# A chunked delta-rule block: the 16x16 diagonal blocks in one strided transfer each way, and their inversion placed ahead of other VectorE work

## The reference

```
l_mat = where(strict, (kbeta @ k.T) * decay, 0)
a_mat = eye(CHUNK) + l_mat
sol   = triangular_solve(a_mat, [v * beta, kbeta * exp(gcum)], lower, unit_diagonal)
v_new = u - w @ state
o     = q_dec @ state + qk @ v_new
state = state * g_last + k_dec.T @ v_new
```

```
o_a = rms_norm(o_a) * silu(z);   mix = concat(o_a, o_b) @ w_out
x   = x + rms_norm(mix);         h = rms_norm(x)
```

## Time and profile before

| | us |
|---|---|
| median of 3 runs | 1429.09 (1427.49 to 1430.75) |
| the profiled execution | 1428.89 |
| its span | 1427.1 |
| of it `mix`, about | 278 to 680 |
| PE busy over the span | 1287.3 (90%) |
| DVE busy | 709.1 (50%) |
| ACT busy | 398.0 (28%) |
| POOL busy | 150.8 (11%) |

### The profile page before, as it was taken

One profiled execution on the slowest core, in us unless ns is written; L12 is line 12 of the kernel. 1 busy time (PEld: TensorE's weight loads), 2 busy tenths in 40 slices (PEclk: granted clock), 3 DMA queues, 4 the chain that ended last, 5 costly groups with the idle time before them and its releaser, 6 DMA issues.

```text
span 1427.1 us, 17527 instructions
## 1 busy us (share of the span) xinstructions
PE 1287.3 (90%) x6360; PEld 1088.5 (76%) x6360; DVE 709.1 (50%) x1075; ACT 398.0 (28%) x744; POOL 150.8 (11%) x184
## 2 busy tenths in 40 slices
PE   5899999647588988878899999999999999999995
PEld 4788888537577878776688888888888888888884
DVE  5232444324756655652653544536362635445358
ACT  5121222235334434422442122122212121221312
POOL 1121000021222123211300000000000000000005
PEclk9999999867699999999899999999999999999998
DMA  7220322272113223112311101011111101010123
GB/s 237 99 100 38 105 74 76 67 266 70 64 38 100 85 97 98 40 47 94 103 60 58 59 29 59 33 56 58 59 42 46 59 29 59 29 59 29 42 91 133
DMA packets 80650, 106.65 MB, mean 75 GB/s; under 512 B 17727, under 2 KB 62559, under 8 KB 80607
## 3 DMA queue, kind: packets, MB, share of 16 engines
q1 hardware_dynamic: 80607, 106.09, 22.4%
HBM read 82.97 MB, written 23.10 MB: 74 GB/s over the span
## 4 chain that ended last, share of the span: by engine, by line
PE 49%; POOL 1%; DVE 1%; issue 1%; ACT 0%; POOLq 0%
PE f_ps_up L2074 11%; PE f_ps_up L2075 11%; PE f_ps_up L2076 11%; PE sums L2092 5%; PE sums L2093 5%; PE sums L2094 5%; POOL stage L1801 1%; POOL f_conv L1801 0%; DVE split L1999 0%; POOL f_stat L2058 0%; DVE f_w_lo L1940 0%; ACT f_w_hi L1872 0%; POOLq L1708 0%; DVE f_conv L2012 0%; DVE h_t L1992 0%
## 5 line engine op out<-in xcount | busy, mean ns | idle before, releaser
L2074 PE MATMUL f_ps_up<-split,f_w_hi 128*128 128x512 f32 x704 | 275.7, 392 | 2.8 <-DVE split L1999 2.8
L2075 PE MATMUL f_ps_up<-split,f_w_hi 128*128 128x512 f32 x704 | 275.3, 391 | 0.0
L2076 PE MATMUL f_ps_up<-split,f_w_lo 128*128 128x512 f32 x704 | 275.1, 391 | 0.0
L1945 DVE SCALAR_TENSOR_TENSOR f_conv<-f_ps_up,f_taps,f_conv 128x1023 f32<-128x1023 f32 x88 | 112.8, 1281 | 275.2 <-ACT f_conv L1876 269.7
L2074 PEld LDWEIGHTS f_ps_up<-split,f_w_hi 128*128 128x128 f32 x704 | 132.9, 189 | 31.4 <-DVE split L1999 2.0
L2076 PEld LDWEIGHTS f_ps_up<-split,f_w_lo 128*128 128x128 f32 x704 | 133.0, 189 | 27.7
L2075 PEld LDWEIGHTS f_ps_up<-split,f_w_hi 128*128 128x128 f32 x704 | 133.0, 189 | 27.5
L1876 ACT ACTIVATE f_conv<-f_ps_up,f_taps 128x1024 f32<-128x1024 f32 x44 | 53.1, 1208 | 326.1 <-PE f_ps_up L2076 326.1
L1957 DVE TENSOR_TENSOR h_t<-sums,h_t 128x512 f32<-128x512 f32 x176 | 116.2, 685 | 37.3 <-PE sums L2094 37.2
L2092 PE MATMUL sums<-f_w_hi,f_y_hi 128*128 128x512 f32 x320 | 124.5, 389 | 0.0
L2093 PE MATMUL sums<-f_w_lo,f_y_hi 128*128 128x512 f32 x320 | 124.5, 389 | 0.0
(11 more groups left out here) (274 smaller groups left out, 2060.0 us busy)
## 6 DMA issues: line engine op xcount, KB each, us to landing
stage<-in_w_up SPq DMA_DIRECT2D x22, 1024.0 KB, 5.1
stage<-in_w_down SPq DMA_DIRECT2D x11, 1024.0 KB, 4.9
raw<-in_w_in SPq DMA_DIRECT2D x6, 1024.0 KB, 6.3
qkv<-xin SPq DMA_DIRECT2D x11, 512.0 KB, 3.2
rows<-row SPq DMA_DIRECT2D x8, 644.0 KB, 3.2
stage<-rows SPq DMA_DIRECT2D x8, 644.0 KB, 5.4
xin<-in_x SPq DMA_DIRECT2D x8, 512.0 KB, 4.8
raw<-in_w_in SPq DMA_DIRECT2D x8, 512.0 KB, 5.6
```

The costliest lines, as they stand in the source:

```text
L1945: op = dve.scalar_tensor_tensor(conv[:, q, k:S], ps_up[:, q % 2, 0:S - k], taps[:, bass.ds(ct + (FTAPS - 1 - k) * 2 * FT, 1)], conv[:, q, ...
L2074: pe.matmul(bank, hi, h_hi[:, k, cols], start=(k == 0), stop=False)
L2075: pe.matmul(bank, hi, h_lo[:, k, cols], start=False, stop=False)
L2076: op = pe.matmul(bank, lo, h_hi[:, k, cols], start=False, stop=(k == KD - 1))
```

## The change

1. `on_diagonal` now describes the diagonal blocks of all four heads in one access pattern. For this the scratch tensors are laid out by head (128x128 numbers of a head, then a gap of 128), so that whole tiles go in and out in pieces of 128 numbers (512 bytes) instead of 512 (2 KB). `load_blk` is one transfer instead of four, `store_xs` two instead of eight.
2. The one count for all of `store_xs` and the one for `load_inv` become two each: blocks may be stored after operation 16, turned blocks after 17; `a_off` waits for `inv` only, and the first `a_inv` for `inv_t`.
3. On VectorE `solve` stands right behind `a_add` of level 6, with `c_out` of the first half between its parts 1 and 2. `b_state` and `b_o`, `d_norm`, `a_qk`, `a_bv` and the second `c_max` come behind it. `d_lo` stands ahead of the first `c_max`. On ScalarE `d_hi` stands ahead of `a_turn` of level 5.
4. In `ffn`, the eight loads of the residual count on two semaphores (four each) instead of four (two each).

```diff
-        def on_diagonal(m, h):
-            pitch = BASE * H * P + BASE
-            return m[0:NB * pitch].rearrange("(b a) -> b a", a=pitch)[:, 0:BASE * H * P].rearrange(
-                "b (r h j) -> b r h j", h=H, j=P)[:, :, h, 0:BASE]
+        def on_diagonal(m):
+            return m[0:H * NB * (BASE * P + BASE)].rearrange("(g a) -> g a", a=BASE * P + BASE)[:, 0:BASE * P].rearrange(
+                "g (r j) -> g r j", j=P)[:, :, 0:BASE]
+        def whole(m):
+            return m.rearrange("(h a) -> h a", h=H)[:, 0:P * P].rearrange("h (p j) -> p h j", j=P)
...
             def load_blk(u):
-                ready((low_out, u, 16), (xs_out, u - 1, 128))
-                for h in range(H):
-                    sp.dma_start(blk[h * NB:(h + 1) * NB, 0:BASE * BASE].rearrange("p (r c) -> p r c", c=BASE),
-                                 on_diagonal(scratch["low"], h)).then_inc(blk_in.sem, 16)
+                ready((low_out, u, 16), (xs_out, u - 1, 16), (xs_t_out, u - 1, 16))
+                sp.dma_start(blocks_of(blk), on_diagonal(scratch["low"])).then_inc(blk_in.sem, 16)
             def store_xs(u):
-                ready((solved, u, SOLVE), (inv_in, u - 1, 32))
-                for m, blocks in ((scratch["inv"], blk), (scratch["inv_t"], products)):
-                    for h in range(H):
...
+                ready((solved, u, SOLVE - 1), (inv_in, u - 1, 16))
+                sp.dma_start(on_diagonal(scratch["inv"]), blocks_of(blk)).then_inc(xs_out.sem, 16)
+                ready((solved, u, SOLVE), (inv_t_in, u - 1, 16))
+                sp.dma_start(on_diagonal(scratch["inv_t"]), blocks_of(products)).then_inc(xs_t_out.sem, 16)
             def load_inv(u):
...
+                ready((xs_out, u, 16), (level, u - 1, L_INV[6]))
+                sp.dma_start(inv[:], whole(scratch["inv"])).then_inc(inv_in.sem, 16)
+                ready((xs_t_out, u, 16), (full["b0"], u - 1, 2))
+                sp.dma_start(inv_t[:], whole(scratch["inv_t"])).then_inc(inv_t_in.sem, 16)
...
                 if a:
+                    solve(t + 1, (0, 1))
+                    c_out(t + 1, 1 - par, 0)
+                    solve(t + 1, (2,))
+                if b:
+                    b_state(t, par)
+                    b_o(t)
                 if e:
                     d_norm(t - 2)
...
             def a_inv(t, n):
                 if n == FIRST:
+                    after(pe, inv_t_in, t)
...
-        s_xr = [sem(f"f_xr{n}") for n in range(T // 2)]
+        s_xr = [sem(f"f_xr{n}") for n in range(2)]
```

More of the change, by code:

```diff
@@ L667, in mix_block @@
         solved = tally("solved", SOLVE)
-        low_out, blk_in, xs_out, inv_in = tally("low_out", 16), tally("blk_in", 64), tally("xs_out", 128), tally("inv_in", 32)
+        low_out, blk_in = tally("low_out", 16), tally("blk_in", 16)
+        xs_out, xs_t_out, inv_in, inv_t_in = (tally(n, 16) for n in ("xs_out", "xs_t_out", "inv_in", "inv_t_in"))
         st_set, o1_set, o_set = tally("st_set"), tally("o1_set"), tally("o_set")
@@ L705, in corners @@
                 "p g (i j) -> p g i j", j=BASE)
-        def on_diagonal(m, h):
-            pitch = BASE * H * P + BASE
-            return m[0:NB * pitch].rearrange("(b a) -> b a", a=pitch)[:, 0:BASE * H * P].rearrange(
-                "b (r h j) -> b r h j", h=H, j=P)[:, :, h, 0:BASE]
-        scratch = {n: nc.dram_tensor(n + "_blocks", (P * (H * P + 1),), F32, kind="Internal").ap() for n in ("low", "inv", "inv_t")}
+        def on_diagonal(m):
[3 more added lines that the diff above has]
+            return m.rearrange("(h a) -> h a", h=H)[:, 0:P * P].rearrange("h (p j) -> p h j", j=P)
+        scratch = {n: nc.dram_tensor(n + "_blocks", (H * (P * P + P),), F32, kind="Internal").ap() for n in ("low", "inv", "inv_t")}
         w_rows = io["w_out"].rearrange("o (k p) n -> p (o k) n", p=P)
@@ L778, in store_x @@
                 sp.dma_start(res_flat[bass.ds(at, P * D)].rearrange("(p n) -> p n", p=P), x[:]).then_inc(x_out.sem, 16)
+            blocks_of = lambda m: m[:, 0:BASE * BASE].rearrange("g (r c) -> g r c", c=BASE)
             def store_low(u):
-                ready((low_set, u, 1), (blk_in, u - 1, 64))
-                sp.dma_start(tile_of(scratch["low"]), flat(low[:])).then_inc(low_out.sem, 16)
+                ready((low_set, u, 1), (blk_in, u - 1, 16))
+                sp.dma_start(whole(scratch["low"]), low[:]).then_inc(low_out.sem, 16)
@@ L797, in load_inv @@
+                ready((solved, u, SOLVE), (inv_t_in, u - 1, 16))
+                sp.dma_start(on_diagonal(scratch["inv_t"]), blocks_of(products)).then_inc(xs_t_out.sem, 16)
             def load_inv(u):
-                ready((xs_out, u, 128), (level, u - 1, L_INV[6]), (full["b0"], u - 1, 2))
-                sp.dma_start(flat(inv[:]), tile_of(scratch["inv"])).then_inc(inv_in.sem, 16)
-                sp.dma_start(flat(inv_t[:]), tile_of(scratch["inv_t"])).then_inc(inv_in.sem, 16)
+                ready((xs_out, u, 16), (level, u - 1, L_INV[6]))
@@ L821, in _ @@
             for m in (scratch["inv"], scratch["inv_t"]):
-                sp.dma_start(tile_of(m), flat(state[:])).then_inc(s_load, 16)
+                sp.dma_start(whole(m), state[:]).then_inc(s_load, 16)
             sp.wait_ge(s_load, LOADS)
@@ L1107, in step @@
                     a_dect(t + 1, 1 - par)
+                if d:
+                    d_hi(t - 1)
                 if b:
                     a_turn(t, 5)
-                if d:
-                    d_hi(t - 1)
                 if e:
@@ L1213, in solve @@
                     after(dve, blk_in, u)
-                    after(dve, xs_out, u - 1)
+                    after(dve, xs_t_out, u - 1)
                     then(dve.memset(blk[:].rearrange("p (r a) -> p r a", a=BASE + 1)[:, :, 0], 1.0), 1)
@@ L1386, in step @@
                     a_low(t + 1, 1 - par)
-                    c_max(t + 1, 0)
                 if d:
                     d_lo(t - 1)
+                if a:
+                    c_max(t + 1, 0)
                 if b:
@@ L1399, in step @@
                 if a:
-                    c_out(t + 1, 1 - par, 0)
                     a_qk(t + 1)
                     a_bv(t + 1, 1 - par)
[L1403 to L1407, removed]
                     c_max(t + 1, 1)
-                    solve(t + 1, (2,))
                 if b:
@@ L1797, in residual @@
             eng.wait_ge(s_norm, t + 1)
-            eng.wait_ge(s_xr[t // 2], 32)
+            eng.wait_ge(s_xr[t // 4], 64)
             if t >= T - 2:
@@ L1861, in _ @@
             for t in range(4, T):
[L1862 removed]
+                sp.dma_start(res_tile(t), io["res"][t]).then_inc(s_xr[t // 4], 16)
             for t in range(T):
```

6 lines of the change are left out of this document (2 added, 4 removed).

## The result

| | before | after |
|---|---|---|
| device time, median | 1429.09 us | 1413.55 us |
| range of five runs | 1427.49 to 1430.92 | 1408.22 to 1417.64 |
| profiled execution: its time; its span; mean granted clock | 1428.9; 1427.1; 0.951 | 1413.55; 1411.7; 0.954 |

The ratio is 0.9889, with an interval of 0.9859 to 0.9919. The change is faster by 15.5 us, where 30 were forecast. 1413.6 lies 8.6 us above the forecast's own range (1391 to 1405) and just above the wide one (1391 to 1413).

What follows compares the result with a forecast made beforehand. In `mix`, TensorE's waits were taken as the limit, worst for the inverse blocks. Steps -1 to 1 +0.3, 2 to 5 -18.1, 6 -3.9, 7 -8.7: -30.4 from 1428.9, so 1399 us; own range 1391 to 1405, wide 1391 to 1413.

Steps and rivals of the forecast that it cites:

- The wait for the inverse blocks: In steady steps of `mix`, TensorE's wait at `a_off` and the lowered clock behind it go: gain 4.3 us.
- Level 4: In steady steps, a new TensorE wait of 0.9 us ahead of `a_trinv`: loss 0.9.
- `d_lo`: TensorE's wait of 1.45 us for `d_lo` goes in steady steps, but L1515 comes only 1.0 earlier: gain 1.0.
- steps 6 and 7: Step 6 of `mix` was to shorten by 3.9 us, and step 7, without part a, by 8.7.
- The blocks in steps 2 to 5: VectorE waits only 0.1 to 0.2 us for the blocks at `solve`, upper bound 1.3; these steps gain 18.1 together.
- late blocks: Rival: `load_blk` with 512 pieces is slow, each microsecond past 2.2 to landing costing the step one: 1440 us, chance 0.04.
- The lowered clock: Rival: new TensorE waits of 0.9, 0.8 and 0.5 us keep the clock low in six steps: 1409 us, chance 0.14.
- The crowded VectorE: Rival: VectorE becomes the bound from `a_low` to the second `c_max`, each step losing 1 to 2 us: 1408, chance 0.10.
- The start: Steps -1 to 1 of `mix`: +5.0 us in step -1, -3.7 in step 0, -1.0 in step 1, together +0.3.
- The loss of 0.5 by `d_out`: In steady steps, `d_out` behind a later second `c_max` and `c_exp` makes `c_pt` and the next squares 0.5 us late.

Runs made afterwards that it cites:

- the transfers alone: The kernel after with VectorE and ScalarE in the order of the kernel before, keeping the new transfers and their counts: 1404.3 us, ratio 0.982.
- the first experiment: The kernel after with SP issuing `store_low` and `load_blk` ahead of `load_qkv` and `load_row`: 1392.8 us, ratio 0.9756.
- the change with one load behind: The kernel after with only `load_row` moved behind `store_low` and `load_blk`, `load_qkv` left in front: 1399.6 us, ratio 0.98.
- with `d_norm` ahead: The kernel after with `d_norm` put back right behind `a_add` of level 6, ahead of `solve`: 1403.2 us, ratio 0.9828.
- the order alone: The kernel before with the change's order on VectorE and ScalarE, its transfers kept as before: 1416.8 us, ratio 0.991.

## Why the prediction was half right

**The wait for the inverse blocks: right.** `store_xs` and `load_inv` end up far ahead of `a_off`. SP and TensorE at the end of step 4, of the kernel after:

```profile
532.62 0.33 SPq L794 DMA_DIRECT2D inv_blocks<-m_blk  x1
533.21 0.33 SPq L796 DMA_DIRECT2D inv_t_blocks<-m_products  x1
536.19 0.38 SPq L800 DMA_DIRECT2D m_inv<-inv_blocks  x1
536.83 0.38 SPq L802 DMA_DIRECT2D m_inv_t<-inv_t_blocks  x1
...
543.65 1.06 PE L1505 MATMUL m_ps_a<-m_inv,m_low_t 128*128 128x128 f32 x8
```

In the earlier trace rows the last load was issued at +43.5 of its step, here at +34.9. L1505 waits for nothing, and the lowered clock of the earlier trace rows behind it is gone. That the transfers alone would do it, I had not seen.

**Level 4, `d_lo`, steps 6 and 7: right.** The new wait of `a_trinv` (L1531) was forecast at 0.9 and is 0.57 in step 5, 0.7 at most. `d_lo`'s wait is gone. Step 6 gains 4.8 (3.9 forecast) and step 7 8.7 (8.7 forecast). In step 7 it is the working too that came out: from its start to the product of level 6 (L1519, at 628.92) it takes 11.3 us, as added up. In step 6 no `load_qkv` and no `load_row` is issued, the store lands in 2.3 us, and the forecast holds there; that alone points at the loads.

**The blocks in steps 2 to 5: the step that failed.** "The blocks must be there: `load_blk` is issued about +14.3." I priced the landing of the load (2.2 us, measured 1.9 to 2.0) and took the landing of `store_low` from the kernel before, with the gap of 3.9 us that stood there in step 4 between it and `load_row`. The trace of the kernel before had the warning: in steps 2 and 3 the store is issued 2.5 us behind `load_row` and lands in 3.6 us, not 2.0. Nothing waited for it there. The change itself moved `m_low` 4.9 us forward in the step and closed that gap to 1.8. `load_blk` is issued at +17.0 in step 4. With the loads behind it, it is issued at +14.3 (503.81 from 489.51), the forecast's number, and the step takes 36.5 where 37.5 was forecast. So the terms of the sum hold to 1 us a step, and one is mis-sized: a wait for the blocks of 0.1 to 0.2 us was 5.59, 3.06, 3.03 and 2.32 us in steps 2 to 5, 14.0 together. The first experiment's kernel has 2.7 there, 11.3 less; its TensorE is busy for 139.1 us in the four steps where the windows above add up to 145.5, 6.3 less, which is the lowered clock. These two make 17.6 us, next to the 17.3 between 164.9 and 147.5. The forecast was 150.0.

**The rivals.** I wrote of late blocks "No small transfer in the steady steps takes that long", and gave them 0.04. It was the right mechanism at the wrong transfer: SP's order has two waits in a row between `m_low` and `solve`, and I looked at the second. And its price was too low: it had a microsecond of the step for each microsecond of landing, and with the lowered clock it was 1.5 (17.3 us for 11.3). The lowered clock came back too, though not behind several small waits, as that rival had it, but behind one of 3 us and more. The crowded VectorE is not it: it has the same 24.5 us of work in a step of 36.5 as in one of 40.9.

**The start: the size was off.** The forecast had +0.3 up to step 2, and it is +2.1. Of that, 0.95 is there before `mix` begins: SP's last transfers of `project` (L258), where nothing was changed, start at 276.73 instead of 275.78, and over the eleven kernels traced this varies between 275.67 and 277.05. In step -1 the 0.7 us from one issue instead of four did come (1.95 us from `load_blk` to the memset, 2.81 before), but behind that later start the memset is at 320.05, no earlier than the 320.04 of the earlier trace rows. Step 0 starts 5.9 later (5.0 forecast), 5.0 with the 0.95 off. In step 1 L1505 starts at 381.94, 3.0 behind the earlier trace rows's 378.90. With the old order in this one step `b_ks` of step 0 starts at 329.1.

**The loss of 0.5 by `d_out`** did not appear: in steps 3 to 5 of the first experiment TensorE's waits of 0.5 us and more are those at L1637 and L1531 alone, and the steps, 36.3 to 36.5, are 1 us below the forecast's 37.5.

## What to carry to other kernels

When an edit makes an early part of a step faster, read again what now stands just ahead of its transfers on the queue: a store that had 4 us of distance from the large loads had 2 afterwards, and its landing went from 2 to 5 us, with its old form (4.2) as with its new one. Order a queue by who is waiting: put the small transfer on the critical path ahead of the large loads for the tile after next. And count every transfer of a chain (store, then load) with a row of its own, under the conditions that it will have after the change.

## What the runs showed of the hardware

In steps 2 to 6 a 256 KB store took 2.0 to 2.3 us to land with nothing large just ahead of it, 2.0 to 2.5 when issued 3.7 to 3.9 us behind `load_row`, 3.6 when issued 2.5 us behind it (both the kernel before), and 4.4 to 7.6 when issued 1.5 to 2.0 us behind `load_row` and its companion `load_qkv`, 1.4 MB together (the kernel after). All of them were issued by SP; whether a store issued by another engine would be spared was not run.

Not every late landing is due to the large loads. In step 1 the store took 3.9 to 4.0 us in four kernels: the change, the change with one load behind, and the two with SP's order altered and VectorE's old. In the last two no large load had been issued for some 40 us. In the seven other kernels it took 2.0 to 2.3. In those four, and in none of the seven, a packet of 16 KB of the kind "instruction" starts between the store's issue and its landing (at 394.30 in the kernel after, whose store was issued at 393.41), and the store ends with a microsecond or more in which the DMA share is 0.04 to 0.07; one engine of the 16 is 0.06. Step 2 of the kernel after has the same: the packet at 433.08, a share of 0.06 from 435.0 to 436.8, and a landing of 7.6 us, 2.5 more than the same gaps gave with `d_norm` ahead. Such a packet (430.13) is also there while the blocks are loaded in step 2 of the first experiment. So some 2.5 of the 14.0 us of waits for the blocks has this beside it. But in step 3 of the kernel after the packet (475.29) stands beside a landing hardly longer than that of step 4 (5.2 to 5.0). That it holds the store up in the cases named is likely, and not shown: no run was made for it.

A single transfer of 512 pieces of 64 bytes landed in 1.9 to 2.0 us. Four of 128 pieces needed 2.7 to 3.0 from the first issue (the order alone), in step 4 some 1.7 from the last.

The length of one wait of TensorE did not decide whether its clock fell. With 2.56 us (L1504 with the transfers alone, window of step 2 above), 2.76 us (L1637 in step 2 of the first experiment) and 3.02 us (L1637 in step 4 with `d_norm` ahead) the clock stayed at 1.00, with 2.61 us and 2.20 (L1531 in step 0 of the kernel after) it fell to 0.50. The four waits of 3.06 us and more at L1637 in the kernel after were followed by 0.50, the one of 0.8 in step 6 was not. What tells the cases in between apart is open; no run was made for it.
